# Four operand tensors of a matmul-bound encoder kernel are moved in SBUF: other distances between streamed and stationary operands

## The reference, cut to what matters

```python
for l in range(DEPTH):                                    # DEPTH = 2
    x = x + 0.5 * swiglu(rmsnorm(x, ffn1_norm[l]), ffn1_w_gate[l], ffn1_w_up[l], ffn1_w_down[l])
    x = x + hybrid_mixer(rmsnorm(x, mix_norm[l]), w_in[l], ...)   # h @ w_in, attention + GLA, @ w_out
    x = x + 0.5 * swiglu(rmsnorm(x, ffn2_norm[l]), ffn2_w_gate[l], ffn2_w_up[l], ffn2_w_down[l])
return rmsnorm(x, final_norm)
# swiglu: silu(x @ w_gate) * (x @ w_up) @ w_down, with w_gate, w_up (1024, 2816), w_down (2816, 1024)
```

## Time and profile before

| | |
|---|---|
| median of 3 runs | 974.51 us (973.07 to 976.95) |
| profiled execution | 971.3 us, its span (first to last instruction) 969.5 us |
| mean granted TensorE clock | 0.995 of full speed |
| matmuls, busy | 8156, 950.8 us (98% of the span) |
| VectorE, ScalarE busy | 617.2 us (64%), 456.6 us (47%) |
| DMA | 169.13 MB, mean 174 GB/s |

### The profile page before, as it was taken

How to read it: one execution, slowest core, us unless ns; L and a number is a source line. 1 busy time by engine, 2 the same in 40 slices (tenths; PEclk the granted TensorE clock), 3 DMA queues, 4 the chain that set the end, 5 groups by cost and what they waited for, 6 DMA issues and landing times.

```text
span 969.5 us, 20036 instructions
## 1 busy us (share of the span) xinstructions
PE 950.8 (98%) x8156; PEld 942.1 (97%) x8156; DVE 617.2 (64%) x729; ACT 456.6 (47%) x489; POOL 11.4 (1%) x13
## 2 busy tenths in 40 slices
PE   7999999999999999999999999999999999999996
PEld 7999999999899999999999999999989999999996
DVE  7755555587768655555686555567796785565553
ACT  5444344457646444344453433436674544434432
POOL 4000000000000000000000000000000000000000
PEclk9999999999999999999999999999999999999998
DMA  7756555644335656556546565564623665655621
GB/s 253 243 185 200 179 176 187 202 139 146 88 128 195 220 178 185 202 173 204 166 160 216 180 209 173 191 199 133 211 51 88 218 217 174 201 189 176 200 100 44
DMA packets 130620, 169.13 MB, mean 174 GB/s; under 512 B 3216, under 2 KB 116112, under 8 KB 130576
## 3 DMA queue, kind: packets, MB, share of 16 engines
q1 hardware_dynamic: 130576, 168.52, 54.5%
HBM read 167.46 MB, written 1.05 MB: 174 GB/s over the span
## 4 chain that ended last, share of the span: by engine, by line
issue 97%; DMA 1%; POOL 1%; PE 0%; DVE 0%; SPq 0%; POOLq 0%; DVEq 0%
DMA raw<-in_ffn_w_gate 1%; POOL sq L1349 0%; PE ps L736 0%; DVE sq L1341 0%; SPq L284 0%; POOLq L98 0%; SPq L287 0%; PE ps L414 0%; POOL sq L1358 0%; POOL sqsum L1349 0%; DVEq L98 0%; DVE rs_y L1033 0%; DVE rs_a L1031 0%; DVE rs_a L1030 0%; SPq L286 0%
## 5 line engine op out<-in xcount | busy, mean ns | idle before, releaser
L980 DVE TENSOR_TENSOR wlo<-raw,whi 128x2048 fp32r<-128x2048 f32 (+1 forms) x159 | 356.0, 2239 | 256.8 <-ACT whi L750 256.7
L357 PE MATMUL ps<-xhi,whi 128*128 128x256 f32 x1696 | 477.2, 281 | 6.8 <-DVE wlo L996 5.2
L358 PE MATMUL ps<-xlo,whi 128*128 128x256 f32 x1696 | 475.0, 280 | 0.0
L359 PE MATMUL ps<-xhi,wlo 128*128 128x256 f32 x1696 | 474.0, 279 | 0.0
L750 ACT ACTIVATE whi<-raw 128x2048 fp32r<-128x2048 f32 (+1 forms) x159 | 297.2, 1869 | 172.9 <-PE ps L359 163.0
L357 PEld LDWEIGHTS ps<-xhi,whi 128*128 128x128 f32 x1696 | 319.3, 188 | 9.3 <-issue 5.4
L358 PEld LDWEIGHTS ps<-xlo,whi 128*128 128x128 f32 x1696 | 318.9, 188 | 0.0
L359 PEld LDWEIGHTS ps<-xhi,wlo 128*128 128x128 f32 x1696 | 318.4, 188 | 0.0
L357 PE MATMUL ps<-h_parts,whi 128*128 128x256 f32 x768 | 213.2, 278 | 0.0
L358 PE MATMUL ps<-h_parts,whi 128*128 128x256 f32 x768 | 213.1, 277 | 0.0
L359 PE MATMUL ps<-h_parts,wlo 128*128 128x256 f32 x768 | 213.0, 277 | 0.0
(11 more groups left out here) (142 smaller groups left out, 476.1 us busy)
## 6 DMA issues: line engine op xcount, KB each, us to landing
raw<-in_ffn_w_down SPq DMA_DIRECT2D x44, 1024.0 KB, 4.9
raw<-in_ffn_w_up SPq DMA_DIRECT2D x43, 1024.0 KB, 5.4
raw<-in_ffn_w_gate SPq DMA_DIRECT2D x42, 1024.0 KB, 5.4
raw<-in_w_in SPq DMA_DIRECT2D x12, 1024.0 KB, 5.2
raw<-in_w_in SPq DMA_DIRECT2D x8, 512.0 KB, 4.5
raw<-in_w_out SPq DMA_DIRECT2D x8, 512.0 KB, 4.3
raw<-in_w_in SPq DMA_DIRECT2D x2, 1088.0 KB, 5.1
raw<-in_ffn_w_gate SPq DMA_DIRECT2D x8, 256.0 KB, 7.2
```

The lines of the kernel that those rows point to most:

```text
L357: pe.matmul(o, w_hi, x_hi, start=start, stop=False, skip_group_check=True)
L358: pe.matmul(o, w_hi, x_lo, start=False, stop=False, skip_group_check=True)
L359: return pe.matmul(o, w_lo, x_hi, start=False, stop=stop, skip_group_check=True)
L980: nc.vector.tensor_tensor(lo, r, h.bitcast(F32), ALU.subtract).then_inc(lo_done, 1)
```

## The change

Four small tensors that nothing reads or writes are put among the SBUF tensors, of 192, 128, 128 and 192 bytes a partition, and `h_parts` becomes two tensors, `h_his` (upper parts) and `h_los` (lower parts). No instruction is added, removed or moved; the operands' addresses differ.

```diff
+        sb("gap_xhi", [P, 48])
         xhi = sb("xhi", [P, KT, SEQ], F32R)
+        sb("gap_xlo", [P, 32])
         xlo = sb("xlo", [P, KT, SEQ], F32R)
...
-        h_parts = sb("h_parts", [P, 4, FT, SEQ], F32R)
-        hhi = [h_parts[:, i] for i in range(2)]
-        hlo = [h_parts[:, 2 + i] for i in range(2)]
+        sb("gap_hhi", [P, 32])
+        h_his = sb("h_his", [P, 2, FT, SEQ], F32R)
+        sb("gap_hlo", [P, 48])
+        h_los = sb("h_los", [P, 2, FT, SEQ], F32R)
+        hhi = [h_his[:, i] for i in range(2)]
+        hlo = [h_los[:, i] for i in range(2)]
...
-        at_parts = h_parts[:, :, :, :].rearrange("p (a b) f t -> p a (b f) t", a=2)
-        mixhi = [at_parts[:, 0, k, :] for k in range(4)] + [xhi[:, k, :] for k in range(4, KT)]
-        mixlo = [at_parts[:, 1, k, :] for k in range(4)] + [xlo[:, k, :] for k in range(4, KT)]
+        at_his, at_los = (h[:, :, :, :].rearrange("p b f t -> p (b f) t") for h in (h_his, h_los))
+        mixhi = [at_his[:, k, :] for k in range(4)] + [xhi[:, k, :] for k in range(4, KT)]
+        mixlo = [at_los[:, k, :] for k in range(4)] + [xlo[:, k, :] for k in range(4, KT)]
```

More of the change, by code:

```diff
@@ L902, in mix @@
                     act.wait_ge(am_done, 4 * l + b + 1)
-                    mixed_hi(at_parts[:, 0, 2 * b:2 * b + 2, :], at32[:, 2 * b:2 * b + 2, :])
+                    mixed_hi(at_his[:, 2 * b:2 * b + 2, :], at32[:, 2 * b:2 * b + 2, :])
                 for b in range(2):
@@ L1262, in mix @@
                     two = slice(2 * b, 2 * b + 2)
-                    mixed_lo(b, at_parts[:, 1, two, :], at32[:, two, :], at_parts[:, 0, two, :])
+                    mixed_lo(b, at_los[:, two, :], at32[:, two, :], at_his[:, two, :])
                 dve.wait_ge(oss_done, ev)
```

## The result

Over 8 runs each, the changed kernel takes a median of 980.17 us (977.36 to 982.14), the kernel before 974.16 (970.44 to 978.76). The ratio is 1.006, with a 95% interval of 1.0035 to 1.0084. The forecast was 952, on the other side. The profiled execution took 979.79 us, its span 978.0.

What follows compares the result with a forecast made beforehand. TensorE's matmul count times start-to-start pace was taken to bound the kernel. x matmuls 22.4 us less, h, token projections and small matmuls nothing: 974.5 - 22.4 = 952.1, rounded 952 us; range 938 to 982.

Steps and rivals of the forecast that it cites:

- What bounds the kernel, and that pace is all: TensorE, 98% busy, hardly waits; time is number of matmuls times start-to-start pace, 117.8 or 113.4 ns.
- That distance matters at all: FFN gate and up units against M_V0, the token projection: same tensors, distance sign turned, 117.8 against 113.2 ns.
- The rule of two independent read ports: Skill's rule: loading weights takes no read bandwidth from the running matmul, so the change does nothing, 974.5 us; chance 0.20.
- The prediction's estimate of 56 us less: All 7392 x and h matmuls coming to the skill's warm pace of 109.2 ns for 256 columns.
- I order the cases by when the two readers meet: Weight minus stream modulo 512: 64 and 320 seen fast, 448 slow; so places between 64 and 320 are fast.
- the 22.4 us that the sum gave to x: 5088 matmuls streaming xhi or xlo, each 4.4 ns faster, 22.4 us less.
- The h term: 2304 matmuls streaming h: bounds 2.7 us less (all fast) to 7.4 more (all slow); taken as no change.
- The token projections: Their 192 matmuls get new distances too: between nothing and 0.8 us more, taken as nothing.
- x stays slow and h loses its fast mode: Rival: x matmuls keep the slow pace, all h matmuls become slow; 7.4 us more, 982 us; chance 0.05.
- The case of bad multiples of 128: Rival: distances that are multiples of 128 cost 3 ns a matmul; 994 us, or 1002 without h's fast mode; chance 0.15.
- wrong first step: Sign: the 96 matmuls of a gate and an up unit take 11.3 us again, or 11.5 and more, not 10.9.
- lost fast mode: Sign for h: the 48 matmuls of a down unit take 5.65 us in place of 5.45.

Runs made afterwards that it cites:

- x256_h384: Kernel before with other gaps: xhi and xlo at distance 256 from the weights modulo 512, both h parts at 384; 993.7 us against 972.2.
- only_x: Kernel before with the change's move of x alone (xhi at distance 256, xlo at 384), h kept at 192; 977.99 us, ratio 1.0031.
- all_shifted: Kernel before with a 64-byte gap ahead of raw, so weights, x and h all move and every distance stays; 974.4 us against 976.1.
- x192_h64: Kernel before with the distances exchanged: xhi and xlo at 192 from the weights modulo 512, both h parts at 64; 965.9 us against 972.2.
- x448_h448: Kernel before with gaps that put all x and h parts at distance 448 from the weights modulo 512; 960.89 us, ratio 0.9858.
- x192_h192: Kernel before with gaps that put all x and h parts at distance 192 from the weights modulo 512; 959.16 us, ratio 0.9832.
- kick_once: x448_h448 with one extra one-column matmul per FFN, ahead of its loop, 4 in all; 954.47 us, ratio 0.9804 to the kernel before.
- kick: x448_h448 with an extra one-column matmul at the start of each of the 36 inner-loop groups; 961.9 us against 973.7 for the kernel before.
- kick_64_192: Kernel before (x at distance 64, h at 192) with the one-column matmul at the start of each of 36 groups; 984.3 us against 973.6.

## Why the prediction was wrong, step by step

- **What bounds the kernel, and that pace is all.** Right. Paces times counts, with the stretches at half clock, account for most of the differences between profiled executions (x256_h384: 5088 x 2.1 + 2304 x 4.1 + 0.6 + 1.7 = 22.4 us, the spans differ by 22.4). In kernels without a break up to 3 us are left over (only_x), and where over 1 us is, the first down unit of the program began 0.9 to 3.3 us later than before. Even at 954 us the largest idle entry of the x matmuls, behind `wlo`, was 8.4 us against 6.8.
- **That distance matters at all.** Right, and now shown with a control: all_shifted keeps the paces, the others change them. The rule of two independent read ports (the Trainium skill, "TensorE: Matmul & The Clock Gate", Step-by-step: what each phase is for) leaves no room for a distance, and is not borne out for this pair of streams: the same 256 and 128 columns take 113.3 to 120.0 ns by distance. Where in the memory the two meet, no run shows. The prediction's estimate of 56 us less (the Trainium skill, the same page, Back-to-back issue gap) put a gap that the page gives for isolated matmuls on a stream with a weight load ahead of each; the best pace in any run was 113.3 ns, not 109.2.
- **The step that failed: "I order the cases by when the two readers meet".** I put three points on a circle of 512 and took the places between the two fast ones to be fast. Two runs put both parts of a tensor at such a place: h at 320 went at 117.8 ns and x at 256 at 120.0. The circle has 256. On it M_V0's distance of 448 and h's of 192 are the same point, and x's of 64 another. There were two points, not three, and nothing to interpolate. The changed kernel's 256, 384, 128 and 320 fall into the classes 0, 128, 128 and 64, none of which has the fast pace. So the 22.4 us that the sum gave to x came to nothing. Its two parts in different classes gave 117.8, less than the 120.0 and about 118.7 that these classes give alone; why they do better in a mixture is open.
- **The h term.** I took "no change" between 2.7 us less and 7.4 more. It was 5.8 more, near the upper bound: h left the one class with the fast pace. The token projections, taken at nothing, cost 0.6 more, as M_V0 left that class too.
- **The rivals.** "x stays slow and h loses its fast mode" is nearest to what happened: 982 forecast, 980.2 measured, and I had given it 0.05. That the number is so close is partly luck: h did not fall to 117.8 but to 117.1, and x stayed at 117.8 only because its two parts, slower in their classes alone, were mixed. I took h's second mode for a detail, though it was nearly all that the change could lose. The case of bad multiples of 128 is true of distances in steps of 64 taken alone, at 1 to 2 ns instead of 3, but the mixture hid it.
- **What the profile after would show.** 11.3 us for the 96 matmuls was named as the sign of a wrong first step, 5.65 for the down unit as that of a lost fast mode (5.62 came). The durations of the x matmuls rose by 1 ns or more (282 at L362 against 281) where they were to fall. The chain was to stay over 95% "issue" and became 92% PE, without a new wait that would explain the pace.

What stays open: what in the memory repeats with 256 bytes; why the class of 192 has two paces and the others one; and what at a break decides which it will be. It need not be chance: the slow FFN is the first of layer 1 in four of the five traced programs with one slow FFN and no break (x192_h64, x448_h448, x192_h192, all_shifted), and the first of layer 0 in the kernel before. Behind one break an FFN, at that place, all four FFNs were at 113.3 at distance 448, in the profiled execution, and the kernel's six executions lie within 3.8 us (953.2 to 957.0) where those of x192_h192 spread over 12 (950.2 to 962.0); before's distances with 36 breaks show that a break alone doesn't ensure it.

## What to carry to other kernels

When TensorE never waits and has a weight load behind every matmul (here 256 columns streamed and 128 float32 columns loaded), read the pace from start to start, stage by stage: two paces for one shape mean that something other than the shape sets it. Then sweep the distance between streamed and stationary tensors in steps of 64 bytes before trusting any argument about which is good; here such kernels led from a change that loses 0.6% to distances that gain 1.4 to 1.7%, and to 2.0% with one break an FFN. Before moving operands, ask first which stage already has the good pace and would lose it.

## What the runs showed of the hardware that was not expected

- The pace of matmuls with 256 streamed and 128 loaded columns depends on the distance of the operands modulo 256 bytes: 119.8 to 120.0 ns at 0, 117.8 at 64, 118.6 to 118.8 at 128, 113.3 or 117.8 at 192, and 116.6 to 120.0 at the odd multiples of 32. Shifting all operands together by 64 left the mean paces as they were. This holds where both parts share a class. In mixtures the neighbours count as well: x at 256 and 384 went at 116.8 or 117.8, h at 192 beside it (only_x) at 117.7 to 117.9 in all four FFNs.
- At distance 192 there are two stable paces, 113.33 and 117.8 ns. A stretch keeps the one it has for over 1500 matmuls, across changes of unit and tensor. A matmul with a single streamed column between two units turned it from 117.8 to 113.3 in three FFNs of kick_once and two of kick. With x at 64, kick_64_192, such a break in every group had h at 113.5 and 117.7 in turns.
- A stretch of 3.4 us at half clock fell into the mixer of layer 0 or 1, within 2 us behind 16 matmuls in a row with one streamed column, in 14 of the 17 profiled executions. The kernel before's was one of the three without it.
